# Last attention with values held in the array and outputs turned, modulation tiles taken out of the first attention, its side tiles cut in two

## The reference

```python
# first layer: 16 heads of 64, each frame attends to its own and all earlier chunks
mod = cond @ ada_w[i] + ada_b[i]               # shift, scale, gate; twice each
s = jnp.einsum('bihd,bjhd->bhij', qc, kb) + bias
p = jax.nn.softmax(s, axis=-1)
o = jnp.einsum('bhij,bjhd->bihd', p, vb)

# hybrid layer: 8 query heads in 2 key groups, three branches, each with a gate
o_cmp = einsum(masked_softmax(qc . kc), vc)    # 31 compressed keys per group
o_slc = einsum(masked_softmax(qr . k_slc), v_slc)
o_win = einsum(masked_softmax(qr . k_win), v_win)
attn = (g[..., 0:1] * o_cmp + g[..., 1:2] * o_slc + g[..., 2:3] * o_win) * silu(z_a)
y = gelu(s5(u)); y = y * sigmoid(y @ glu_w + glu_b)
x = x + gate * (concat([attn, y * silu(z_s)]) @ w_out)
```

## Time and profile before

| | |
|---|---|
| median of 3 runs | 1852.87 us (1850.45 to 1854.12) |
| the profiled execution | 1851.63 us, span 1849.5 us |
| PE / DVE / ACT busy over the span | 95% / 63% / 36% |
| first attention, about | 166 to 278 us of the span |
| last attention, about | 1606 to 1746 us |
| state-space blocks and output | 1746 us to the end |

### The profile page before, as it was taken

One profiled execution on the slowest core, in us unless ns is written; L12 is line 12 of the kernel. 1 busy time (PEld: TensorE's weight loads), 2 busy tenths in 40 slices (PEclk: granted clock), 3 DMA queues, 4 the chain that ended last, 5 costly groups with the idle time before them and its releaser, 6 DMA issues.

```text
span 1849.5 us, 24233 instructions
## 1 busy us (share of the span) xinstructions
PE 1762.0 (95%) x9361; PEld 1465.6 (79%) x9361; DVE 1164.7 (63%) x2372; ACT 669.3 (36%) x1081; POOL 101.9 (6%) x194
## 2 busy tenths in 40 slices
PE   3999989999999999999999999999999999899999
PEld 2777659888888888878888889888888977677787
DVE  6876684876467655655454448875587479545574
ACT  3323573523242334232131325322323332366432
POOL 0001110001000100100000000010001100000000
PEclk9999999999999999999999999999999999999999
DMA  9354331335333525552424223445345322300351
GB/s 366 115 181 161 125 104 69 143 132 169 141 114 114 185 100 174 195 181 85 144 71 147 79 103 125 156 141 187 127 144 182 118 91 91 134 27 20 138 197 46
DMA packets 45470, 245.98 MB, mean 133 GB/s; under 512 B 6256, under 2 KB 6480, under 8 KB 27440
## 3 DMA queue, kind: packets, MB, share of 16 engines
q1 hardware_dynamic: 24848, 155.36, 23.3%
q0 software_dynamic: 20512, 89.11, 14.3%
HBM read 229.23 MB, written 15.22 MB: 132 GB/s over the span
## 4 chain that ended last, share of the span: by engine, by line
PE 80%; DVE 12%; ACT 3%; issue 2%; DMA 2%; SPq 0%; DVEq 0%; ACTq 0%
PE ps L472 69%; DVE w_lo L1474 2%; PE ps L929 2%; DVE ada_raw L1498 1%; PE ps L803 1%; PE ps L910 1%; DMA ada_raw<-in_ada 1%; ACT w_hi L1044 1%; PE ps L919 1%; DVE ada_first L1856 1%; PE ps L651 1%; PE ps L665 1%; PE ps L642 1%; DVE a_p L1958 1%; PE ps L951 1%
## 5 line engine op out<-in xcount | busy, mean ns | idle before, releaser
L1474 DVE TENSOR_TENSOR w_lo<-w_raw,w_hi 128x2048 fp32r<-128x2048 f32 x136 | 311.6, 2291 | 153.7 <-ACT w_hi L1044 153.4
L1044 ACT ACTIVATE w_hi<-w_raw 128x2048 fp32r<-128x2048 f32 x136 | 260.1, 1912 | 361.2 <-PE ps L472 338.4
L472 PE MATMUL ps<-h_hi,w_hi 128*128 128x512 f32 (+1 forms) x1008 | 377.8, 375 | 5.8 <-DVE w_lo L1474 2.4
L472 PE MATMUL ps<-h_lo,w_hi 128*128 128x512 f32 (+1 forms) x1008 | 373.4, 370 | 0.0
L472 PE MATMUL ps<-h_hi,w_lo 128*128 128x512 f32 (+1 forms) x1008 | 373.2, 370 | 0.0
L472 PEld LDWEIGHTS ps<-h_hi,w_hi 128*128 128x128 f32 x1008 | 191.5, 190 | 39.1 <-issue 5.0
L472 PEld LDWEIGHTS ps<-h_hi,w_lo 128*128 128x128 f32 x1008 | 191.2, 190 | 32.3
L472 PEld LDWEIGHTS ps<-h_lo,w_hi 128*128 128x128 f32 x1008 | 191.5, 190 | 30.5
L472 PE MATMUL ps<-hid_hi,w_hi 128*128 128x512 f32 (+1 forms) x576 | 211.3, 367 | 0.0
L472 PE MATMUL ps<-hid_lo,w_hi 128*128 128x512 f32 (+1 forms) x576 | 210.5, 366 | 0.0
L472 PE MATMUL ps<-hid_hi,w_lo 128*128 128x512 f32 (+1 forms) x576 | 210.5, 366 | 0.0
(11 more groups left out here) (395 smaller groups left out, 2476.4 us busy)
## 6 DMA issues: line engine op xcount, KB each, us to landing
w_raw<-in_slabs SPq DMA_DIRECT2D x136, 1024.0 KB, 4.8
ada_raw<-in_ada POOLq DMA_DIRECT2D x104, 512.0 KB, 4.7
s_tables<-s_tab POOLq DMA_DIRECT2D x4, 2692.0 KB, 9.2
s_t<-s_tables POOLq DMA_DIRECT2D x4, 2692.0 KB, 9.8
ada_first<-in_ada SPq DMA_DIRECT2D x16, 512.0 KB, 15.2
a_bias<-in_a_bias POOLq DMA_DIRECT2D x16, 256.0 KB, 3.5
xT<-in_xT SPq DMA_DIRECT2D x4, 512.0 KB, 6.2
s_toeplitz<-KTp POOLq DMA_DIRECT2D x32, 64.0 KB, 3.3
```

The lines of the kernel that those rows point to most:

```text
L472: last = mm(o, l, r, start=start and n == 0, stop=stop and n == 2)
L1044: A(w_hi[s][:], w_raw[:, s, :], ACT.Copy).then_inc(sem("hi_done"), 1)
L1474: tt(w_lo[s][:], w_raw[:, s, :], w_hi[s][:].bitcast(F32), ALU.subtract).then_inc(sem("lo_done"), 1)
```

## The change

First attention: of its 16 modulation tiles 8 stay (`A_ADA`, steps 8 to 36). Six go into the tail, two at each of its three slabs, and two into the head of the MLP, ahead of the tables' first stage. POOL's issues follow. The 8 side products start at steps 0, 8, 14, 20, 26, 30, 34, 38 and are each made in two pieces of 12 matmuls, in neighbouring steps. Four outputs are kept instead of three, and are split at steps 41 to 44.

Last attention: the values are made as in the first attention. The 64 columns of `hv` are the weights, the transposed probabilities stream, group 0 writes output partitions 0 to 63 and group 1 partitions 64 to 127, and both branches of a head pair accumulate in one bank. For that the probabilities are multiplied by reciprocal and gate before they are transposed, each pair of units by itself, and the compressed branch's by its own; it accumulates into the same bank (`compressed_out`, at steps 20, 36, 52, 68). So `h_o`, its additions and its 16 transposes fall away, and `h_gate`, `o_hi`, `o_lo` are made from the bank inside the loop. The pipeline is one step deeper up to the transposes, two up to the values. Behind the loop the first part of the output product is done right after `states(0)`.

```diff
-A_EARLY = 3
+A_EARLY = 4
+A_ADA = 8
@@ constants @@
-        SIDE_A, SIDE_H = Side([4 * u for u in range(2 * TT)], TT), Side([1, 11, 22, 33, 44, 55], 2)
-        A_KEPT = [32 + 2 * i for i in range(A_EARLY)]
+        SIDE_A, SIDE_H = Side([0, 8, 14, 20, 26, 30, 34, 38], TT, 2), Side([1, 11, 22, 33, 44, 55], 2)
+        A_KEPT = [41 + i for i in range(A_EARLY)]
-        CMP_STEPS = {step: (n // 3, n % 3) for n, step in enumerate((6, 9, 13, 23, 27, 31, 35, 38, 41, 46, 50, 57))}
-        CMP_ADD = {16 * i + 22: i for i in range(4)}
+        CMP_STEPS = {step: (n // 2, n % 2) for n, step in enumerate((6, 13, 23, 31, 35, 41, 46, 52))}
+        CMP_SCALE = {step + 4: i for step, (i, part) in CMP_STEPS.items() if part == 0}
+        OUT_STEPS = {16 * i + 20: i for i in range(4)}
+        ATT_PARTS = (1,), (2, 3), (4, 5), (6,)
@@ POOL @@
-            for h in range(A_HEADS + 2):
...
+            for h in range(A_HEADS):
...
+                if 2 <= h < A_ADA + 2:
                     ada(16 + ADA_QKV + h - 2, 16 + ADA_QKV + h - 1)
+            ada(16 + ADA_QKV + A_ADA, ADA_TILES)
@@ PE, last attention @@
-                u = s - 4
-                if 0 <= u < NUH:
-                    i, it, br, g = UNITS_H[u]
-                    pe.wait_ge(sem("hpt_ready"), u + 1)
...
-                    for j in range(it + 1):
-                        last = mm(o, h_pt[:, u % 3, j * P:(j + 1) * P], hv[:, j, vc], start=j == 0, stop=j == it)
+                u = s - 6
+                if u >= 0 and s % 2 == 0:
+                    i, it, br, _ = UNITS_H[u]
+                    pe.wait_ge(sem("hpt_ready"), u + 2)
+                    if u % 16 == 0 and i >= 2:
+                        pe.wait_ge(sem("hxo_gated"), i - 1)
                     for j in range(it + 1):
+                        for g in range(H_GROUPS):
+                            vc = slice((br - 1) * P + g * HD, (br - 1) * P + (g + 1) * HD)
+                            last = mm(ps[5 + i % 2][HD * g:HD * g + HD, it * P:(it + 1) * P], hv[:, j, vc],
+                                      h_pt[:, (u + g) % 4, j * P:(j + 1) * P], start=it == 0 and br == 1 and j == 0, stop=False, skip_group_check=True)
                     last.then_inc(sem("ho_full"), 1)
+                if s in OUT_STEPS:
+                    compressed_out(OUT_STEPS[s])
@@ PE, behind it @@
             states(0)
-            pe.wait_ge(sem("h_added"), 4)
-            for i in range(4):
-                transposes([h_o[:, t, i * P:(i + 1) * P] for t in range(TT)], "hxo_full")
+            attention_part(0)
@@ DVE, head of the MLP @@
                             if o == 4:
+                                if layer == 0:
+                                    ada(2, 0)
+                                    ada_put()
                                 beside(0)
@@ DVE, first attention and its tail @@
-                if s >= 8 and s % 4 == 0 and q < NUA // 4:
+                if s >= 8 and s % 4 == 0 and q < A_ADA:
                     ada(1, 0)
...
-            tail(16)
+            tail(16, lambda s: ada(2, 0))
@@ DVE, last attention @@
+                u = s - 3
+                if 0 <= u < NUH and s % 2:
+                    i, it, br, _ = UNITS_H[u]
+                    n, h2 = P * (it + 1), slice(u % 8, u % 8 + 2)
+                    dve.wait_ge(sem("he_done"), u + 2)
+                    step(V.reciprocal(row_inv[:, h2], row_sum[:, h2]))
+                    step(tt(h_w[:, h2], row_inv[:, h2], h_gts[:, it, 6 * i:6 * i + 6].rearrange("p (g b) -> p g b", b=N_BR)[:, :, br], ALU.mult))
+                    for v in (u, u + 1):
+                        ts_(h_p[:, v % 6, 0:n], h_p[:, v % 6, 0:n], h_w[:, v % 8:v % 8 + 1], None, ALU.mult).then_inc(sem("hp_ready"), 1)
+                if s - 2 in OUT_STEPS:
...
+                    tt(h_gate[:, i % 2, :], ps[5 + i % 2][:], za[:, i, :], ALU.mult).then_inc(sem("hxo_gated"), 1)
+                if s - 4 in OUT_STEPS:
...
+                    tt(o_lo[:, i, :], h_gate[:, i % 2, :], o_hi[:, i, :].bitcast(F32), ALU.subtract).then_inc(sem("hx_done"), 1)
```

More of the change, by code:

```diff
@@ L168, in program @@
         hv = at("hv", 44 * K, [P, TT, 256])
-        h_p = at("h_p", 48 * K, [P, 5, T])
-        h_pt = at("h_pt", 58 * K, [P, 3, T])
-        h_o = at("h_o", 72 * K, [P, TT, 512])
+        h_p = at("h_p", 48 * K, [P, 6, T])
+        h_pt = at("h_pt", 60 * K, [P, 4, T])
+        h_gate = at("h_gate", 68 * K, [P, 2, T])
+        o_hi = at("o_hi", 72 * K, [P, 4, T], F32R)
+        o_lo = at("o_lo", 0, [P, 4, T], F32R)
         h_qn = at("h_qn", 48 * K, [P, TT, 512])
@@ L348, in program @@
         ZA_READ = len(SIDE_A.starts) + 1 + H_USES.index(SIDE_H.starts[1]) + 1
+        C_COPIED = [len(SIDE_A.starts) + 1 + H_USES.index(step) + 1 for step, (i, part) in CMP_STEPS.items() if part == 1]
         SIDE_ALL = len(SIDE_A.starts) + 1 + len(H_USES)
@@ L891, in compressed @@
                     last.then_inc(sem("c_full"), 1)
-                elif part == 1:
-                    pe.wait_ge(sem("c_exp"), i + 1)
+                else:
+                    pe.wait_ge(sem("c_scaled"), i + 1)
                     for h in range(2):
@@ L896, in compressed, with compressed_out @@
                     last.then_inc(sem("c_turned"), 1)
-                else:
-                    for h in range(2):
-                        last = mm(ps[7][:, 256 * h:256 * h + 256], c_pt[:, h, :], vblk[:], start=True, stop=True)
-                    last.then_inc(sem("c_out"), 1)
-            for s in range(NUH + 4):
+            def compressed_out(i):
+                pe.wait_ge(sem("side_free"), C_COPIED[i])
+                for it in range(TT):
+                    last = mm(ps[5 + i % 2][:, it * P:(it + 1) * P], vblk[:, it % 2, :], c_pt[i % 2][:, it // 2, :],
+                              start=False, stop=True, skip_group_check=True)
+                last.then_inc(sem("c_out"), 1)
+            for s in range(NUH + 5):
                 if s < NUH and s % 2 == 0:
@@ L1381, in place_z @@
                 return za[:, 2 + u, :] if u < 2 else zs[:, u - 2, :]
-            for s in range(NUH + 3):
+            for s in range(NUH + 8):
                 side(SIDE_H, s, place_z)
@@ L2175, in _ @@
             dve.wait_ge(sem("gts_done"), 1)
-            for s in range(NUH + 7):
+            for s in range(NUH + 9):
                 if s < NUH:
@@ L2198, in _ @@
                     V.engine_nop().then_inc(sem("side_free"), 1)
-                if s - 1 in CMP_STEPS:
-                    i, part = CMP_STEPS[s - 1]
+                if s - 1 in CMP_STEPS and CMP_STEPS[s - 1][1] == 0 or s in CMP_SCALE:
+                    i, part = (CMP_SCALE[s], 1) if s in CMP_SCALE else CMP_STEPS[s - 1]
                     cs = c_s[:].rearrange("p (j n) -> p j n", n=CMP_PAD)
@@ L2298, in _ @@
             recurrence(0)
[L2299 to L2311 removed]
+            attention_part(0)
+            free(V.engine_nop(), 4)
+            c.add("bank", 4)
             for blk in range(NBLK):
@@ L2315, in _ @@
                     recurrence(blk + 1)
[L2316 to L2319 removed]
+                for o in ATT_PARTS[blk]:
+                    attention_part(o)
                 turned_y(blk)
```

184 lines of the change are left out of this document (68 added, 116 removed).

## The result

The changed kernel takes 1857.3 us (median of 12 runs, 1853.52 to 1860.85) against 1853.38 before: a ratio of 1.0020, interval 1.0012 to 1.0027. It is 3.9 us slower. The forecast was 1845, with 1853 as the upper end; the measurement lies between the third rival (1850) and the fourth (1863.8).

The account below looks back on a forecast made before the run. PE was taken to bound the last attention nearly everywhere, and the first except some twelve us of waiting. 1851.6 - 5.5 - 2.2 - 2.7 + 4.2 = 1845.4 us, predicted as 1845, range 1833 to 1853.

Parts of the forecast that it names:

- the third rival: DVE's chain eats the last attention's whole saving and the first attention yields 3 us: 1850 us, chance 0.20.
- the fourth: Last attention: reciprocal, product and first multiplication, 0.70 us, delay each of 32 pairs: 1863.8 us, chance 0.10.
- the stage of the last attention: Last attention, scores of unit 0 to `states`: values, transposed-copy waits, DVE waits and longer pipeline sum to 2.2 us gained.
- The values' price: Last attention: half-width values save PE 11.5 us, dearer transposes take 9.6, 2.9 come back; 5 us gained.
- The waits for `h_pt`: Last attention: PE's two waits for the transposed copy, 2.0 us, go, as values stand two steps behind transposes.
- The scaling from the first attention's 11.3 us: Last attention: PE's waits for DVE's multiplied probabilities, scaled by DVE's queued work to 10 us, taken as 4 us lost.
- The chain's rival: Last attention: DVE's chain delays every pair, deciding from a 0.34 us wait per pair; 1863.8 us, chance 0.10.
- The first attention: First attention: moving 8 of 16 modulation tiles out and spreading the side products gains 5.5 us, ends 1 and 9.
- the head: Head of the first MLP: two added tiles delay a transfer and PE's low part; 4.2 us lost, ends 0.5 and 5.5.
- The tiles' 4.5: First attention: the modulation tiles' leaving gains 3.7 us of waits and 0.8 us of drain.
- the division's 1 us: First attention: side pieces of 12 and 12 matmuls instead of 24 let DVE deliver before PE asks; 1 us gained.
- The boundary: Behind the last attention: DVE's recurrence starts earlier, so the second block's `outputs` follow sooner; 2.7 us gained, ends 0 and 4.

Follow-up runs that it names:

- wide weights: The changed kernel with 128 columns of `hv`, both groups' at once, instead of 64 as weights of the last attention's values: 1863.4 us (ratio 1.0047).

## Why the prediction was wrong

- **Step that failed: the stage of the last attention, "5 + 2.0 - 4 - 0.8 = 2.2 us gained, ends -6 and +12".** It came out 7.4 us longer in the profile, 9.6 us of the 13.3 by which the two profiles miss the sum; 2.4 us more are the row ahead of it, which is luck. The terms, from the rows above: PE's own work 129.7 to 122.1, 7.6 us less; idle 7.5 to 14.9, 7.4 more; half clock 132.7 - 129.7 = 3.0 before and 132.7 - 122.1 = 10.6 after, 7.6 more. So the saving came, and the waits and the clock each took it back once.
- **The values' price was right in kind, too small by 2.6 us.** 5 us of PE's work were forecast and 7.6 measured, if the compressed branch is even, as the prediction took it. Up to 0.10 us of a transpose group's extra goes with wide weights. With the Trainium skill's rule in TensorEngine Tiling (Array Packing), section Tiling Modes, that changing the mode drains the engine, the wide-weight run agrees (0.26 to 0.16 us for one transpose). The up to 2x of that page's section Theoretical Speedup is there for a pass (0.11 to 0.055), not for the stage.
- **The idle time was forecast 2.8 us longer and was 7.4.** The waits for `h_pt` stay (3.0 us). The waits for `h_p` are 5.6 us, not 4, half of them by the order of two blocks in DVE's queue. The scaling from the first attention's 11.3 us gave 10 us, was cut to 4 by an argument with no row behind it, and named no place; the order of the queue was readable and was not read.
- **The clock was not in the sum.** No term and no rival had it. The chain's rival (0.34 us per pair as the turning point) speaks of waits alone; 0.18 us per pair of waits for `h_p`, 0.23 of all added idle time, sufficed, because the half clock added in the stage costs as much as the waits added there. Shown: filling three waits takes 3.2 and 3.9 us off two versions, and the rows go to 1.00. Not shown is how the 7.6 us divide among the waits, of which two of the three filled ones are in the kernel before too. The signs that the prediction gave for being wrong (waits past 11 us, no wait in the head, a stage shorter by over 12 us) all stayed away: they watched the waits, and none the clock.
- **The first attention (-5.5, measured -6.6) and the head (+4.2, measured +5.1) were right, the shares inside not.** The tiles' 4.5 and the division's 1 us are 2.6 and 0.9 apart, and the rest is theirs together. In the head DVE waited 1.53 us for the transfer (2.5 forecast) and PE 2.95 for the low part (4.2); that the sum came near is luck, for 1.7 us of half clock, which it didn't have, made up most of the difference.
- **The boundary (-2.7) and the tail (0) were right.**
- The sum started from an execution of the kernel before with a clock of 0.990, against a median of 0.988, and the lucky 114.7 us in it; it lies 1.8 us under the median of the 12 runs. The range allowed for the terms' ends, not for that.

## What to carry to other kernels

A wait of a tensor engine that is otherwise full is to be priced twice, once for itself and once for the half clock that may follow it; where a wait can't be taken away, some unused products in it may pay. In an engine's queue, put the work that a full engine waits for ahead of the work that only has to be done some time: exchanging two blocks brought 3.2 us here (2.4 by the ratios). And of work that is moved, the place decides: six tiles were free in one place, and two cost 5 us in another, where DVE waited for a transfer in front of what PE needed.

## What was not expected of the hardware

- Nine products of no use, 256 columns each, make the program 3.2 and 3.9 us shorter (2.6 and 3.0 by the ratios); six more, in the wait of 2.06 us, another 1.2 us (within the spread).
- Twelve runs of one kernel differ by 4 to 13 us, and most of that goes with the granted clock (the changed kernel's go from 1853.52 us at 0.987 to 1860.85 us at 0.979, nearly in order).
- The half clock costs little where it falls on a wait or just ahead of one: 2.4 us between two profiles of the same code.
